# A seventh pair of expert units outside the weight ring, and the last expert's sums in another order

## The reference

```python
combine = ...              # two experts a token, both out of the best of four groups
for e in range(N_EXPERTS):
    h = jax.nn.silu(t @ w_gate[e]) * (t @ w_up[e])    # 2048 -> 512
    y = y + combine[:, e:e + 1] * (h @ w_down[e])     # 512 -> 2048
```

## Time and profile before

| | |
|---|---|
| runs | 1707.85, 1711.0, 1715.21 us; median 1711.0 |
| profiled execution | 1711.18 us, its span 1709.4 us |
| PE busy | 1573.0 us, 92% of the span |
| DVE, ACT, POOL busy | 668.2, 432.5, 29.4 us |
| DMA | 531.17 MB, mean 311 GB/s |
| mean granted TensorE clock | 0.973 |

### The profile page before, as it was taken

The page is one execution under the profiler, slowest core; times in us unless marked ns, Lnnn a source line. Parts: engine busy times, 40 slices in busy tenths (PEclk is TensorE's granted clock), DMA queues, the critical chain, the costliest instruction groups (busy, mean ns, idle before and its releaser), DMA issues.

```text
span 1709.4 us, 19027 instructions
## 1 busy us (share of the span) xinstructions
PE 1573.0 (92%) x7841; PEld 918.8 (54%) x7841; DVE 668.2 (39%) x937; ACT 432.5 (25%) x551; POOL 29.4 (2%) x26
## 2 busy tenths in 40 slices
PE   7999999997999999899859999998899989999993
PEld 6888776875343343243238878786434335334331
DVE  5445335535123232223174474455323223223316
ACT  5334335325110111010034453333211101101112
POOL 0010000000000000000022000000000000000000
PEclk9999999997999999999979999998899999999997
DMA  8574323545999999999976464456599998999993
GB/s 348 193 255 173 127 96 129 216 172 208 417 427 428 428 426 429 429 427 427 428 320 246 174 240 177 140 180 246 210 429 427 427 427 364 420 384 428 429 427 152
DMA packets 47315, 531.17 MB, mean 311 GB/s; under 512 B 5361, under 2 KB 5905, under 8 KB 7938
## 3 DMA queue, kind: packets, MB, share of 16 engines
q1 hardware_dynamic: 45234, 518.08, 74.4%
q0 software_dynamic: 2000, 11.95, 1.9%
HBM read 527.91 MB, written 2.10 MB: 310 GB/s over the span
## 4 chain that ended last, share of the span: by engine, by line
PE 71%; DMA 20%; DVE 5%; ACT 2%; issue 1%; SPq 0%; POOL 0%; DVEq 0%; ACTq 0%
PE bank L1028 26%; DMA w_all<-in_moe_w_down 19%; PE bank L689 10%; PE bank L691 10%; PE bank L690 10%; PE bank L994 4%; PE bank L1077 2%; PE bank L823 2%; PE bank L1060 1%; PE bank L1007 1%; PE bank L896 1%; PE bank L1117 1%; DVE small L1678 1%; DVE X L2099 1%; ACT X L1327 1%
## 5 line engine op out<-in xcount | busy, mean ns | idle before, releaser
L1028 PE MATMUL bank<-w_all,xg 128*64 128x512 f32 x2048 | 460.1, 598 | 25.6 <-DMA w_all<-in_moe_w_gate_up 23.5
L689 PE MATMUL bank<-w_hi,T_hi 128*128 128x512 f32 x768 | 301.3, 392 | 6.2 <-DVE w_lo L1655 3.8
L1028 PEld LDWEIGHTS bank<-w_all,xg 128*64 128x64 f32 x2048 | 140.5, 137 | 309.5 <-issue 258.6
L691 PE MATMUL bank<-w_hi,T_lo 128*128 128x512 f32 x768 | 299.4, 390 | 0.0
L690 PE MATMUL bank<-w_lo,T_hi 128*128 128x512 f32 x768 | 299.4, 390 | 0.0
L1655 DVE TENSOR_TENSOR w_lo<-w_land,w_hi 128x2048 fp32r<-128x2048 f32 (+1 forms) x96 | 214.2, 2240 | 208.6 <-ACT w_hi L1300 208.6
L2088 DVE TENSOR_TENSOR y_lo<-bank,y_hi 128x512 fp32r<-128x512 f32 x62 | 42.9, 692 | 530.3 <-ACT y_hi L1495 530.3
L1300 ACT CAST w_hi<-w_land 128x2048 fp32r<-128x2048 f32 (+1 forms) x100 | 184.4, 1854 | 244.6 <-PE bank L691 238.6
L2099 DVE SCALAR_TENSOR_TENSOR X<-bank,weight,X 128x512 f32<-128x512 f32 x256 | 174.2, 743 | 51.6 <-PE bank L1077 51.4
L689 PEld LDWEIGHTS bank<-w_hi,T_hi 128*128 128x128 f32 x768 | 144.6, 188 | 37.4 <-issue 3.1
L691 PEld LDWEIGHTS bank<-w_hi,T_lo 128*128 128x128 f32 x768 | 144.4, 188 | 30.4
(11 more groups left out here) (285 smaller groups left out, 1067.7 us busy)
## 6 DMA issues: line engine op xcount, KB each, us to landing
w_all<-in_moe_w_gate_up SPq DMA_DIRECT2D x128, 2048.0 KB, 19.3
w_all<-in_moe_w_down SPq DMA_DIRECT2D x64, 2048.0 KB, 24.2
w_land<-in_ev_w_in SPq DMA_DIRECT2D x32, 1024.0 KB, 4.9
w_land<-in_od_w_in SPq DMA_DIRECT2D x32, 1024.0 KB, 4.8
w_land<-in_ev_w_out SPq DMA_DIRECT2D x16, 1024.0 KB, 4.9
w_land<-in_od_w_out SPq DMA_DIRECT2D x16, 1024.0 KB, 4.8
w_land<-in_att_w SPq DMA_DIRECT2D x7, 1024.0 KB, 4.8
x0T<-in_xT SPq DMA_DIRECT2D x4, 512.0 KB, 6.2
```

The lines of the kernel that those rows point to most:

```text
L689: pe.matmul(dst, hi_l, hi_r, start=start, stop=False)
L691: return pe.matmul(dst, lo_l, hi_r, start=False, stop=stop)
L1028: ins = pe.matmul(dst[halves[h], :], cols(c), U.weights(q, pos + h)[:, c, :], start=start and c == 0, stop=stop and c == 3)
```

## The change

Three edits. (1) The seventh pair of each layer gets a buffer of its own, `early`, over `rt`, `y_hi` and `y_lo` (16 KB a partition; `rt` is moved next to the other two). SP issues it when the router's products are done. From there on every unit stands two places earlier in the ring, and the counts at the end of the ring follow: `stream` waits two units later for the dense block after the experts, and `split(SB_IN1)` for all units of the layer. (2) For the last expert, PE does `scatter(3, 0)` ahead of down pair 1, in banks 0, 1, 4 and 5, and `scatter(3, 1)` in banks 6, 7, 0 and 1; DVE adds (3, 0) and takes the statistics of its first 512 columns before `y_out(3, 1)`. (3) In the layer norm after the experts of layer 0, DVE writes `T_lo` of piece m - 2 after piece m, instead of m - 3.

```diff
+def sum_bank(a, h, final=None):
+    return 4 + 2 * a + h if final is None else ((0, 1, 4, 5), (6, 7, 0, 1))[final][2 * a + h]
...
+        rt = moe_buf("rt", [P, 2, 4, SEQ])
+        early = sb("early", [P, 2, 4 * NB], offset=o3[0] - 4 * 2 * 4 * NB)
...
-        rt = moe_buf("rt", [P, 2, 4, SEQ])
...
+            def is_early(self, q, pos):
+                return isinstance(q, int) and q == 0 and self.index(q, pos) // 2 == 6
+
+            def in_ring(self, q, pos):
+                i = self.index(q, pos)
+                return i if isinstance(q, int) and q == 0 and i < 12 else i - 2
+
             def slot(self, q, pos):
-                return self.index(q, pos) % 12
+                return self.in_ring(q, pos) % 12
...
+                if isinstance(q, int) and q == 0 and i < 26:
+                    return 4 * self.sb0 + i - 14 + 1
                 return PER_QUAD * q + (4 * self.sb0 + i - 12 + 1)
...
-                    sp.wait_ge(used, 4 * freed_by(sb) + j + 1)
+                    sp.wait_ge(used, 4 * freed_by(sb) + j + (3 if SB_MOE0 <= freed_by(sb) < SB_IN1 else 1))
...
+                        if U.is_early(q, pos):
+                            sp.wait_ge(logits_done, 2 * layer + 1)
+                            sp.dma_start(early[:].rearrange("p u n -> p (u n)"), moe_src(layer, at_e, part, j)) \
+                                .then_inc(early_in, 16)
+                            return
...
-                    def scatter(e, p):
+                    def scatter(e, p, final=None):
                         E = 4 * Q + e
                         pe.wait_ge(y_lo_done, 2 * E + p + 1)
-                        ge(pe, acc_done, 8 * E + 4 * p)
+                        if final is None:
+                            ge(pe, acc_done, 8 * E + 4 * p)
                         wide = is_wide(layer, q, e)
                         for a in range(TT):
+                            if final == 0 and a == 1:
+                                pe.wait_ge(acc_done, 8 * E - 2)
+                            if final == 1:
+                                pe.wait_ge(acc_done, 8 * E + 2 * a)
...
-                        down(48, 3, None, lambda: scatter(2, 1))
-                        first_sums(3, None)
-                        scatter(3, 1)
+                        def sums_between():
+                            scatter(2, 1)
+                            pe.wait_ge(slots_out, 4 * Q + 4)
+                            scatter(3, 0, final=0)
+
+                        down(48, 3, None, sums_between)
+                        scatter(3, 1, final=1)
...
-                    ge(act, used, 4 * (sb - 1) + j + 1)
+                    ge(act, used, 4 * sb if count is None and sb == SB_IN1 else 4 * (sb - 1) + j + 1)
...
                         y_out(3, 0)
                         add(2, 1)
+                        add(3, 0, final=0)
+                        statistics(3, 0, (0,))
                         y_out(3, 1)
-                        add(3, 0)
-                        statistics(3, 0)
-                        add(3, 1)
+                        statistics(3, 0, (1,))
+                        add(3, 1, final=1)
                         statistics(3, 1)
...
-                layer_norm((1, 4)[layer], X, x_ready, lambda m: transposed(T_IN1, m - 3) if layer == 0 and m >= 3
+                layer_norm((1, 4)[layer], X, x_ready, lambda m: transposed(T_IN1, m - 2) if layer == 0 and m >= 2
                            else None)
```

More of the change, by code:

```diff
@@ L398, in build @@
         chain_a, chain_v = sem("chain_a"), sem("chain_v")
+        early_in = sem("early_in")
         landed = [[sem(f"landed{g}{j}") for j in range(4)] for g in range(3)]
@@ L486, in used @@
                 return PER_QUAD * q + (4 * self.sb0 + self.index(q, pos) + 1)
+            def is_early(self, q, pos):
[3 more added lines that the diff above has]
+                return i if isinstance(q, int) and q == 0 and i < 12 else i - 2
             def slot(self, q, pos):
-                return self.index(q, pos) % 12
+                return self.in_ring(q, pos) % 12
             def landed(self, q, pos):
-                s, turns = self.slot(q, pos), self.index(q, pos) // 12
-                return landed[s // 4][s % 4], 16 * 4 * q + 16 * (LANDED[self.sb0 + s // 4] + turns + 1)
+                if self.is_early(q, pos):
+                    return early_in, 16 * (1 if self.sb0 == SB_MOE0 else 2)
+                s, turns = self.slot(q, pos), self.in_ring(q, pos) // 12
+                before = LANDED[self.sb0 + s // 4] - (1 if s >= 10 and self.sb0 == SB_MOE1 else 0)
+                return landed[s // 4][s % 4], 16 * 4 * q + 16 * (before + turns + 1)
             def pair_freed(self, q, pos):
@@ L503, in freed @@
                     return 4 * freed_by(self.sb0 + i // 4) + i % 4 + 1
+                if isinstance(q, int) and q == 0 and i < 26:
+                    return 4 * self.sb0 + i - 14 + 1
                 return PER_QUAD * q + (4 * self.sb0 + i - 12 + 1)
             def weights(self, q, pos):
+                if self.is_early(q, pos):
+                    return early[:, self.index(q, pos) % 2, :].rearrange("p (c n) -> p c n", c=4)
                 return w_all[:, self.slot(q, pos), :].rearrange("p (c n) -> p c n", c=4)
@@ L573, in fetch @@
                     def fetch(pos, e, part, j):
+                        at_e = 4 * q + e
+                        if U.is_early(q, pos):
[3 more added lines that the diff above has]
+                            return
                         sp.wait_ge(used, U.pair_freed(q, pos))
                         s = U.slot(q, pos)
-                        at_e = 4 * q + e
                         sp.dma_start(w_all[:, s:s + 2, :].rearrange("p u n -> p (u n)"),
@@ L1076, in scatter @@
                                     rows_h, at_h = (slice(0, ALL), h) if wide else (halves[h], p)
-                                    ins = pe.matmul(bank[4 + 2 * a + h][:], placeT[rows_h, e % 2, a * P:(a + 1) * P],
+                                    ins = pe.matmul(bank[sum_bank(a, h, final)][:], placeT[rows_h, e % 2, a * P:(a + 1) * P],
                                                     (y_hi, y_lo)[k][rows_h, at_h, :], start=k == 0, stop=k == 1)
@@ L2089, in y_out, with add @@
                             .then_inc(y_lo_done, 1)
-                    def add(e, p):
+                    def add(e, p, final=None):
                         E = 4 * Q + e
@@ L2098, in add, with statistics @@
                                 v = X[:, a, n * NB:(n + 1) * NB]
-                                dve.scalar_tensor_tensor(v, bank[4 + 2 * a + h][:], weight[:, e % 4, a:a + 1], v, ALU.mult,
+                                dve.scalar_tensor_tensor(v, bank[sum_bank(a, h, final)][:], weight[:, e % 4, a:a + 1], v, ALU.mult,
                                                          ALU.add).then_inc(acc_done, 1)
-                    def statistics(e, p):
+                    def statistics(e, p, blocks=(0, 1)):
                         dve.wait_ge(acc_done, 8 * (4 * Q + e) + 4 * p + 4)
-                        for n in (2 * p, 2 * p + 1):
+                        for n in (2 * p + h for h in blocks):
                             for a in range(TT):
@@ L2210, in moe @@
                 dve.sem_inc(moe_over, 1)
-                layer_norm((1, 4)[layer], X, x_ready, lambda m: transposed(T_IN1, m - 3) if layer == 0 and m >= 3
+                layer_norm((1, 4)[layer], X, x_ready, lambda m: transposed(T_IN1, m - 2) if layer == 0 and m >= 2
                            else None)
             moe(0)
-            for g in (5, 6, 7):
+            for g in (6, 7):
                 transposed(T_IN1, g)
```

## The result

The changed kernel takes 1695.66 us (median of 4 runs, 1695.18 to 1697.13) against 1710.56 for the kernel before: a ratio of 0.9912, 95% interval [0.9897, 0.9928]. That is 14.9 us, where 18.2 were forecast (1693.0, range 1687.5 to 1700.5). Run again later it was 1697.06 against 1710.03, ratio 0.9916 [0.9898, 0.9934].

What follows compares the result with a forecast made beforehand. Expert stages were taken as bound by DMA, dense stages by PE; gains were sought in hole, tail and dense start. 1711.2 - 9.8 (pairs) - 7.8 (sums) - 0.6 (T_lo) = 1693.0 us, range 1687.5 to 1700.5.

Steps and rivals of the forecast that it cites:

- The early pair: Seventh pair moved in the idle DMA hole of each layer, stream one pair ahead: 4.9 us a layer, 9.8 us together.
- Rival A: Stream's lead lost around pair 13, or too little idle PE: 1697.9 us (one layer, chance 0.08) or 1702.8 (both, 0.04).
- 1.6 us in hand: Pair 13, issued at 447.4 us, could land at 455.1, ahead of the 456.7 when it should land; squeeze costed at 0.
- The shifted ring: Next dense block's units issued one pair later, ACT's first cast waiting for the last down product: cost 0, at most 3.9 us.
- The sums: Last expert's tail: two statistics instead of an add and four statistics after the last y_lo, 3.9 us a layer, 7.8 together.
- SP, ACT and POOL do nothing more: Last expert's tail: the reordered sums give these three engines no extra work; part of the 3.9 us a layer.
- 0.8 us to spare: Layer 0's tail: ACT's casts and table load end at 878.4 us, before the norm's statistics at about 879.2.
- the last of those that the prediction gives for "right": Sign at the dense stage's start: first dense matmul 20.9 us after the last pair instead of 25.7.
- Rival C: The tails give nothing because scatter(3,0) or the earlier add comes too late: 7.8 us stay, 1700.8 us, chance 0.06.
- The clock: PE's clock in layer 1's last down pair: taken as 0, or 1.7 us more gain if it stays up.
- rival B: PE's clock stays up in layer 1's tail, its gap now holding scatter(3,0): 1691.3 us, chance 0.15.
- T_lo: Start of the dense stage: T_lo one piece earlier brings the first matmul 0.7 to 0.9 us forward, 0.6 us kept, once.

## Why the prediction was right, and where it was not

**The early pair: right.** Forecast 4.9 us a layer. Over the seven profiles with it and the five without, issue to last down is 446.06 against 450.80 us in layer 0 and 457.29 against 462.08 in layer 1: 4.7 and 4.8, and in neither layer do the two sets overlap. Rival A did not come: pair 13, with "1.6 us in hand", was issued at 449.7 and landed 8.8 us later, 458.5, right behind pair 12 (442.8 + 10.7 = 453.5). Its wait in the queue was shorter than before and the stream stayed closed. PE's idle time in front of the wide expert was enough.

**The shifted ring: right at 0.** ACT's first cast started at 869.04, after its own landing, 1.2 us behind the end of the last down pair, as computed.

**The sums: right in layer 1, wrong in layer 0.** In layer 1 the tail without the clock's part is 3.95 us shorter, forecast 3.9. In layer 0 it is 0.07. The failed step is in edit 2: "SP, ACT and POOL do nothing more", and with it the 3.9 us taken for layer 0. POOL indeed does nothing more, but what it does lies beside the tail and holds DVE without any semaphore between them. The prediction checked ACT (0.8 us to spare) and the queues, and put POOL at nothing without reading a row of it. DVE was at its tensor_scalar 11.8 us after the last down pair started, POOL at its end after 15.8. It is also where the opening's "meet only at semaphores" does not hold. The sign that failed is the last of those that the prediction gives for "right": the first dense matmul came 24.4 us after the last pair (864.21 to 888.58), not 20.9, while the aggregate, which stands ahead of the held instruction, came after the forecast 11.4. Rival C had the right size of loss for one layer but the wrong cause.

**The clock: rival B's mechanism came true.** The rows decided nothing at 1 of 2; with 5 of 8 against 0 of 16 it is the wide gap that lets the clock fall, though not each time. A fuller gap kept the clock. It is worth 1.4 us a layer on average, and in both layers. With the rule of the Trainium skill ("TensorE: Matmul & The Clock Gate", section "What's actually happening") that the prediction set beside the sum the traces agree in 5 of the 8 wide gaps and in all 16 narrow ones; in the other 3 the clock stayed up.

**T_lo: right sign, mis-sized.** The slip of the transposes was as forecast (they start 7.36 us after the reciprocal before, 7.74 after). But the first dense matmul starts 0.77 us after they start (887.81 to 888.58); the prediction let it wait for their recorded end, 1.1 us. The start moved 1.25 us instead of 0.7 to 0.9. The clock rose 3.7 us after it instead of 2.8 (half of the 0.9 is given back), so about 0.8 was kept, forecast 0.6.

**What the parts make.** 9.5 (pairs) + 4.0 (layer 1's sums) + 2.7 (clock, two tails) + 0.9 (layer 0's 0.07 and T_lo) is 17 us; measured were 14.9 and 13.0. So it is partly luck that the total of 18.2 came as near as it did: 3.8 us of the sums were missing, and the clock, put at 0, gave 2.7 of them back. In the untouched stretch before the first router products, the seven kernels with the early pair reach the last of them at 399.5 us on average, the five without at 396.8. The granted clock from 215 to 232 us is 0.80 or 0.90 in five of the seven and 0.90 in one of the five, and 1.00 in the others. The 2.7 us between them are about what is missing, but whether they are chance or come from edit 1 was not tested and stays open.

## What to carry to other kernels

When a tail is shortened on one engine, look at everything that runs beside it, also what has no semaphore to it: the old tail may have been exactly as long as the neighbour's work. An instruction whose duration jumps, here from 0.17 to 4 us, and that ends with another engine's instruction may be held by it. Move the other's work and see whether the long instruction moves too; then put that work where the held engine waits anyway. A prefetch into a stream that DMA sets was worth its bytes over the rate here (4.7 and 4.8 us of 4.9), with an idle hole to put it in and a consumer that had idle time to give back.

## What the runs showed of the hardware that I had not expected

POOL's tensor_tensor over 2048 columns, 4.5 us each, held DVE instructions of two columns for up to 4.3 us, including a tensor_scalar with one input; statistics and adds with a PSUM input ran beside it at full speed. And 2.6 us of idle PE let the clock fall in 5 of 8 cases, at the end of a stage in which PE had been busy 304.0 of 334.8 us at a granted clock of 1.00.
